# Who makes the sums of activation blocks for a Strassen-like down projection: VectorE or GpSimd

## Chip, cores and metric

The kernel runs on one core of a Trainium2 chip. The metric is the device time of one execution in microseconds (us). TensorE is called PE in the profile (its weight loads PEld), VectorE is DVE, ScalarE is ACT, GpSimd is POOL, SyncE is SP.

## What is computed

One decoder layer in float32, sequence 512, width 1024. Only its last part matters here, the feed-forward half:

```
h = rmsnorm(x);  u = causal depthwise conv3(h @ W_up)
a, b = split(u);  f = gelu(a) * b          # (512, 2816)
x = x + rmsnorm_post(f @ W_down)           # (2816 -> 1024)
```

## The kernel before, in words

**Products.** Every float32 operand of a matmul is split into a high half (rounded by ScalarE into a float32r tile) and a low half (operand minus high half, made by VectorE), and each product is three matmuls (L690 to L694). Both large feed-forward products are cut into 2 x 2 blocks and done with seven block products instead of eight, in a form in which sums and differences of blocks are built one after another. For the down projection the products are numbered 1 to 7. A unit is `(p, g)`: product `p` for the couple of feature tiles `g`, with g from 0 to 5. A couple has two pairs of tiles, the last couple (g = 5) one, so its units are half as long. There are 42 units in the hand-written order `DOWN_UNITS` (L82). The first four of them (`EARLY_DOWN`) stand among the last units of the up projection (`_tail`, L67).

**Weights.** A unit's weights go through one of six raw buffers. SyncE loads block 1 of a chain of sums by a plain transfer (L550, L556). The later members of a chain are made by transfers that add in flight onto what the buffer holds; these are issued from GpSimd's queue (L669 for the up projection, L677 for the down projection), each after VectorE has made the low half of the buffer's contents before (semaphore `w_lo`). ScalarE copies the raw buffer to one of four slots of `ws` (L1367, L1443, semaphore `w_hi`), VectorE subtracts (L1825 up, L1948 down, `w_lo`), TensorE multiplies and frees the slot (`unit_done`). The copies run four units ahead of TensorE.

**Activations.** `fT`, in the tile `work`, holds f in 22 tiles. A share is the operand of one unit, 128x512 (128x256 for g = 5): ScalarE writes its high half (L1434, `f_hi`), VectorE its low half (`f_share_lo`, L1921, `f_lo`). Before each unit TensorE waits for `w_lo` and `f_lo` (L1047, L1048). The operand of products 5, 6, 3 and 7 is not f itself but a sum or difference of blocks of f, built in place in `fT`. Four families of `tensor_tensor` on VectorE, six instructions each, make them:

- `f_difference(g)`, L1943, signals `f_diff`: before product 5;
- `f_sum_of` for p = 5, L1930, `f_sum2`: before product 6, and needed by the next two;
- `f_sum_of` for p = 6, L1934, `f_sum4`: before product 3;
- `f_sum_of` for p = 4, L1938, `f_sum3`: before product 7.

A sum of the last three families may overwrite a block only when the low half of the share before it has been made, so it waits for `f_lo`. `F_EARLY` and `F_DIFF` (L98, L101) say behind which unit of the up projection the first ones stand; `shares_at(n)` (L105) says which shares are split at step n of the down projection. VectorE's step n is: low half of weights n (`down_lo`), then the low halves and the sums of `shares_at(n)`.

**Orders.** Each engine runs its own list in order. GpSimd's list before: first all adding transfers of the up projection, then all of the down projection in the order of `DOWN_UNITS`, then four small row statistics at the end. All semaphores are waits on constants.

Of the kernel before, what the change touches and what calls it, by code (L numbers as in the profile page):

```python
# [32 lines left out]
ALU = mybir.AluOpType  # L33
# [10 lines left out]
FT = DFF // P  # L44
# [9 lines left out]
UP0 = OUT0 + 2 * KT  # L54
# [14 lines left out]
UP_UNITS = [("plain", 0, j) for j in range(4)] + [u for _, u in sorted(_steady, key=lambda e: e[0]) if u not in _tail] + _tail  # L69
UP_AT = {u: n for n, u in enumerate(UP_UNITS)}  # L70
EARLY_DOWN = 4
# [3 lines left out]
UP_ADDS = {7: (1, 0), 6: (1, 1), 3: (0, 1), 5: (1, 0)}  # L75
UP_NEXT = {1: 7, 7: 6, 6: 3, 4: 5}
DOWN0 = UP0 + len(UP_UNITS) - EARLY_DOWN
# [3 lines left out]
COUPLES = 6  # L81
DOWN_UNITS = [(1, 0), (1, 1), (1, 2), (5, 0), (1, 3), (5, 1), (6, 0), (1, 4), (5, 2), (1, 5), (5, 3),  # L82
# [10 lines left out]
STAGE = {p: (c, k) for c, stages in CHAINS.items() for k, (p, _) in enumerate(stages)}  # L93
# [7 lines left out]
F_DIFF = {(2, 4): 0, (2, 6): 1, (5, 7): 2, (5, 8): 3}  # L101
# [3 lines left out]
def shares_at(n):  # L105


    def upto(k):
        return min(9 if k < 9 else max(k, 10) + min(max(k - 11, 0) // 3, 6), len(DOWN_UNITS))

    return range(upto(n - 1), upto(n))
# [9 lines left out]
def raw_of(n):  # L121

    p, g = DOWN_UNITS[n]
    return (4, 5, 3, 0, 2, 1)[CHAIN_ORDER.index((STAGE[p][0], g)) % RAWS]
# [9 lines left out]
def down_n(k):  # L134

    return UP0 + UP_AT["down", k] if k < EARLY_DOWN else DOWN0 + k
# [10 lines left out]
def raw_slot_of(n):  # L147

    kind, i = unit_of(n)[:2]
    if kind == "in":  # L150
        return slot_of(n)
    if kind == "down":
        return raw_of(i)
    if kind == "plain":
        return unit_of(n)[2]
    if kind == 2:
        return 5
    return (2, 3)[i % 2] if kind in (4, 5) else (4, 0, 1)[(i - PLAIN) % 3]
# [13 lines left out]
def loads_of_slot(n):  # L172

    return sum(raw_slot_of(m) == raw_slot_of(n) and is_loaded(m) for m in range(n + 1))
# [7 lines left out]
def before_in_slot(n):  # L182

    return max((m for m in range(n) if raw_slot_of(m) == raw_slot_of(n)), default=None)
# [10 lines left out]
def lo_count(n):  # L195

    if n < POOL_TO:
        return n + 1
    return n + 1 - POOL_TO
# [15 lines left out]
def build(nc, x, norm_mix_pre, w_in, rel_bias, w_out, norm_mix_post, norm_ffn_pre, w_up,  # L215
          conv_w, conv_b, w_down, norm_ffn_post, rotary, decay, onehot, out):
    ctx = ExitStack()
    with ctx:
# [99 lines left out]
        def raw_unit(n):  # L318

            c = raw_of(n)  # L320
            return (late[:, c - 4, :] if c >= 4 else raw[:, c, :])[:, 0:512 * pairs_of(DOWN_UNITS[n][1])]
# [23 lines left out]
        def f_block(g, odd, half):  # L345

            t, w = 4 * g + odd, slice(half * 256, half * 256 + 256)
            return fT[:, t:t + 2 * pairs_of(g) - 1:2, w]
# [39 lines left out]
        raw_loaded = [sem(f"raw_loaded{s}") for s in range(RAWS)]  # L388
# [63 lines left out]
        def up_block(block, i):  # L452

            value, half = block
            return w_up_v[:, 4 * half:4 * half + 4, value * DFF + i * (2 * P):value * DFF + (i + 1) * (2 * P)]

        def up_raw(n):

            c = raw_slot_of(n)
            return late[:, c - 4, :] if c >= 4 else raw[:, c, :]  # L460

        def w_block(p, g):

            odd, right = BLOCK[p]
            t = 4 * g + odd
            return w_down_v[:, t:t + 2 * pairs_of(g) - 1:2, right * 512:right * 512 + 512]
# [101 lines left out]
        def _(pool):  # L568
# [87 lines left out]
            for pair in ((0, 1), (2, 3)):  # L656
                for s in pair:
                    out_rstd(s)
                for s in pair:
                    pool.wait_ge(sq_done, ST + s + 1)  # L660
                    row_rstd(ST + s, sumsq[:, ST + s:ST + s + 1])
            for n, unit in enumerate(UP_UNITS):
                if unit[0] not in UP_NEXT:
                    continue
                p, i = UP_NEXT[unit[0]], unit[1]
                m = UP0 + UP_AT[p, i]
                pool.wait_ge(raw_loaded[raw_slot_of(m)], 16 * loads_of_slot(m))
                pool.wait_ge(w_lo, lo_count(UP0 + n))
                pool.dma_start(up_raw(m).rearrange("p (k n) -> p k n", k=4), up_block(UP_ADDS[p], i),  # L669
                               accum_op=ALU.add).then_inc(raw_added[raw_slot_of(m)], 16)  # L670

            for n, (p, g) in enumerate(DOWN_UNITS):
                if not STAGE[p][1]:
                    continue
                c = raw_of(n)
                pool.wait_ge(w_lo, lo_count(before_in_slot(down_n(n))))
                pool.dma_start(raw_unit(n), w_block(p, g), accum_op=ALU.add).then_inc(raw_added[c], 16)  # L677

            for k, s in enumerate((2, 3, 0, 1)):
                pool.wait_ge(block_sq, (4, 6, 7, 8)[k])  # L680
# [841 lines left out]
        def _(dve):  # L1522
# [389 lines left out]
                nc.vector.tensor_tensor(t_block(p, 1), tF[m], f32(t_block(p, 0)), ALU.subtract).then_inc(t_lo, 1)  # L1912

            def f_lo_of(n):
                f_share_lo(n)
                f_sum_of(n)

            def f_share_lo(n):
                g = DOWN_UNITS[n][1]
                dve.wait_ge(f_hi, n + 1)  # L1920
                nc.vector.tensor_tensor(two(f_unit(n, 1), g), f_operand(n), f32(two(f_unit(n, 0), g)),  # L1921
                                        ALU.subtract).then_inc(f_lo, 1)

            def f_sum_of(n):
                p, g = DOWN_UNITS[n]
                a11, a12, a21, a22 = f_block(g, 0, 0), f_block(g, 1, 0), f_block(g, 0, 1), f_block(g, 1, 1)
                if p == 5:

                    dve.wait_ge(f_lo, n + 1)
                    nc.vector.tensor_tensor(a11, a21, a11, ALU.add).then_inc(f_sum2, 1)  # L1930
                if p == 6:

                    dve.wait_ge(f_lo, n + 1)
                    nc.vector.tensor_tensor(a21, a11, a12, ALU.subtract).then_inc(f_sum4, 1)  # L1934
                if p == 4:

                    dve.wait_ge(f_lo, n + 1)
                    nc.vector.tensor_tensor(a22, a11, a22, ALU.subtract).then_inc(f_sum3, 1)  # L1938

            def f_difference(g):  # L1940

                dve.wait_ge(f_ready, min(4 * g + 4, FT))
                nc.vector.tensor_tensor(f_block(g, 0, 1), f_block(g, 1, 1), f_block(g, 0, 1), ALU.subtract).then_inc(f_diff, 1)  # L1943

            def down_lo(n):
                c, w = slot_of(down_n(n)), 512 * pairs_of(DOWN_UNITS[n][1])
# [56 lines left out]
            for n in range(len(UP_UNITS)):  # L2003
                up_sum(n)
                if unit_of(UP0 + n + AHEAD)[0] == "down":
                    down_lo(unit_of(UP0 + n + AHEAD)[1])
                else:
                    up_split_lo(n + AHEAD)
                up_post(n)
                if n < 4:  # L2010
                    blocks_lo(n)
                if UP_UNITS[n] in F_DIFF:
                    f_difference(F_DIFF[UP_UNITS[n]])
                for m in F_EARLY.get(UP_UNITS[n], ()):
                    if n + 1 < len(UP_UNITS):
                        f_lo_of(m)
# [1 line left out]
            late_share, = F_EARLY[UP_UNITS[-1]]  # L2018
            gate_row(SWEEP - 1, 0)
            gate_row(SWEEP - 1, 1)  # L2020
            f_share_lo(late_share)
            for n in range(AHEAD + EARLY_DOWN, len(DOWN_UNITS)):
                if n == last[6] + 4:
                    e_sums()
                    g_sums()
                if n == AHEAD + EARLY_DOWN + 1:
                    f_tiles(SWEEP - 1)
                down_lo(n)
                if n == AHEAD + EARLY_DOWN + 2:
                    f_sum_of(late_share)  # L2030
                    f_difference(COUPLES - 2)
                if n == AHEAD + EARLY_DOWN + 4:
                    f_difference(COUPLES - 1)
                for m in shares_at(n):
                    f_lo_of(m)
                if n == last[4] + 3:
                    e4_sums()
                    dve.wait_ge(gains3_loaded, 16)
                if n == last[3] + 4:
                    for r in range(2):  # L2040
                        dve.wait_ge(g_done, r + 1)
                        add_block(r, 1, 3, g_sum)
                if n == last[3] + 5:
                    gain(0, 1)
                    gain(1, 1)
                if n == last[7] + 3:
                    for r in range(2):
                        dve.wait_ge(e4_done, r + 1)
                        add_block(2 + r, 0, 7, e_sum)
                        add_block(2 + r, 1, 7, g_sum)  # L2050
                if n == last[7] + 4:
                    gain(2, 0)
                    gain(2, 1)
                if n == last[7] + 5:
                    gain(3, 0)
                    gain(3, 1)
# [60 lines left out]
```

## Time and profile before

| | |
|---|---|
| median of 3 runs | 619.94 us (619.67 to 621.11) |
| the profiled execution | 619.47 us |
| its span in the trace | 617.7 us |
| TensorE busy | 606.2 us, 98% |
| VectorE busy | 473.8 us, 77% |
| ScalarE busy | 364.9 us, 59% |
| GpSimd busy | 143.9 us, 23% |

The up projection's seven-product part runs from about 289 us to 515 us of the span, the down projection from there to 612 us (its first four units lie between 499 and 513 us). The last microseconds are the norm and the stores. A row of a timeline gives start and duration in us, engine, line of the kernel, operation, tiles and shapes; in brackets the idle time of that engine before it and what ended it. Instructions of one engine that follow without a gap overlap by some hundredths of a microsecond, so the distance between two starts is what an instruction takes of its engine's time.

### The profile page before, as it was taken

Reading aid. Unit: us, or ns where it says so; the run is one execution under the profiler, and the core shown is the slowest. Engines: PE = TensorE matmul, PEld = TensorE weight load, DVE = VectorE, ACT = ScalarE, POOL = GpSimd, SP = SyncE. Lnnn points to the kernel's source line nnn. Section 1 sums busy time; section 2 is a strip of 40 time slices with the busy share of each in tenths; the row PEclk is TensorE's granted clock in tenths of the full one; section 3 lists DMA queues with packets and bytes.
Section 4 is the critical chain, followed back from the end, with each engine's and each line's share of the span. In section 5 each row is a group of like instructions: output and inputs, shape, how many; then the busy total and the mean of one; then the engine's idle time right before and its main releaser. Section 6 shows DMA issues by size and latency. Waiting matters only on the chain.

```text
span 617.7 us, 9966 instructions
## 1 busy us (share of the span) xinstructions
PE 606.2 (98%) x3710; PEld 531.5 (86%) x3710; DVE 473.8 (77%) x678; ACT 364.9 (59%) x571; POOL 143.9 (23%) x145
## 2 busy tenths in 40 slices
PE   8999999999999999999999999999999999899996
PEld 8888778788787877889989999999999998688885
DVE  3657548656854985978974598889889899999886
ACT  5558337536743853773844566666666656667661
POOL 4313103111310302312012222222222322522213
PEclk9999999999999999999999999999999999999998
DMA  9834223322422255581467988998899879997933
GB/s 278 239 103 126 86 69 103 102 58 78 135 69 68 102 179 165 186 254 35 103 157 151 177 158 178 210 186 172 154 222 184 184 141 183 162 235 175 233 103 136
DMA packets 87785, 93.27 MB, mean 151 GB/s; under 512 B 3049, under 2 KB 72345, under 8 KB 87746
## 3 DMA queue, kind: packets, MB, share of 16 engines
q0 software_dynamic: 26352, 35.15, 33.6%
q1 hardware_dynamic: 61394, 57.59, 29.2%
q8 instruction: 25, 0.41, 0.3%
q14 instruction: 14, 0.11, 0.1%
HBM read 90.62 MB, written 2.12 MB: 150 GB/s over the span
## 4 chain that ended last, share of the span: by engine, by line
PE 84%; DVE 8%; POOL 2%; issue 2%; ACT 2%; DMA 1%; DVEq 0%; SPq 0%; POOLq 0%; ACTq 0%
PE bank L694 75%; DVE ws L1948 2%; PE bank L774 1%; PE bank L836 1%; PE bank L705 1%; POOL grstd L622 1%; DMA gains<-in_norm_mix_pre_dram 1%; PE bank L825 1%; DVE xs L1649 1%; PE bank L765 1%; PE bank L764 1%; POOL work L626 1%; PE bank L815 1%; DVE work L1819 1%; PE bank L814 1%
## 5 line engine op out<-in xcount | busy, mean ns | idle before, releaser
L694 PE MATMUL bank<-hT,ws 128*128 128x256 f32 (+1 forms) x1656 | 295.3, 332 | 0.7 <-DVE work L1627 0.6
L694 PEld LDWEIGHTS bank<-hT,ws 128*128 128x128 f32 x1656 | 245.7, 190 | 28.2 <-issue 2.5
L694 PE MATMUL bank<-yT,ws 128*128 128x256 f32 x864 | 106.8, 283 | 0.0
L694 PEld LDWEIGHTS bank<-yT,ws 128*128 128x128 f32 x864 | 105.2, 192 | 0.2
L694 PE MATMUL bank<-ws,yT 128*128 128x512 f32 x366 | 86.6, 392 | 2.1 <-DVE yT L1921 2.1
L694 PEld LDWEIGHTS bank<-ws,yT 128*128 128x128 f32 x366 | 67.8, 188 | 16.6 <-DVE ws L1948 2.5
L1367 ACT ACTIVATE ws<-raw 128x1024 fp32r<-128x1024 f32 x46 | 48.7, 1059 | 46.1 <-PE bank L694 46.1
L1825 DVE TENSOR_TENSOR ws<-raw,ws 128x1024 fp32r<-128x1024 f32 x46 | 56.1, 1221 | 15.2 <-ACT ws L1367 15.2
L1529 DVE TENSOR_TENSOR ws<-raw,ws 128x1024 fp32r<-128x1024 f32 x47 | 57.6, 1226 | 5.8 <-ACT ws L1105 5.4
L669 POOL DMA_DIRECT2D raw<-in_w_up_dram x27 | 34.7, 1284 | 108.1 <-DVE ws L1825 103.6
L1105 ACT ACTIVATE ws<-raw 128x1024 fp32r<-128x1024 f32 x48 | 50.7, 1058 | 14.9 <-PE bank L694 10.8
L694 PE MATMUL bank<-ws,hT 128*128 128x512 f32 x240 | 55.6, 389 | 0.0
L694 PEld LDWEIGHTS bank<-ws,hT 128*128 128x128 f32 x240 | 44.9, 188 | 9.2
L1825 DVE TENSOR_TENSOR ws<-late,ws 128x1024 fp32r<-128x1024 f32 x21 | 25.7, 1222 | 16.0 <-ACT ws L1367 16.0
L1443 ACT ACTIVATE ws<-raw 128x1024 fp32r<-128x1024 f32 (+1 forms) x28 | 26.6, 950 | 15.6 <-PE bank L694 14.8
L1367 ACT ACTIVATE ws<-late 128x1024 fp32r<-128x1024 f32 x21 | 22.3, 1060 | 21.9 <-PE bank L694 21.4
L1649 DVE CUSTOM_DVE_ANT_0 xs<-bank,work 128x128 f32<-128x128 f32 (+3 forms) x32 | 14.7, 489 | 25.6 <-PE bank L815 25.4
L1948 DVE TENSOR_TENSOR ws<-raw,ws 128x1024 fp32r<-128x1024 f32 (+1 forms) x28 | 30.4, 1084 | 3.8 <-ACT ws L1443 3.8
L1597 DVE TENSOR_TENSOR work<-bank,work 128x512 f32<-128x512 f32 (+3 forms) x32 | 15.5, 489 | 19.9 <-PE bank L765 19.9
L677 POOL DMA_DIRECT2D raw<-in_w_down_dram x16 | 18.5, 1176 | 33.2 <-DVE ws L1948 33.2
L669 POOL DMA_DIRECT2D late<-in_w_up_dram x9 | 11.7, 1297 | 52.8 <-DVE ws L1825 52.8
L1175 ACT ACTIVATE work<-bank 32x512 f32<-32x512 f32 x32 | 18.9, 591 | 8.5 <-PE bank L694 8.1
(174 smaller groups left out, 794.5 us busy)
## 6 DMA issues: line engine op xcount, KB each, us to landing
raw<-in_w_in_dram SPq DMA_DIRECT2D x28, 512.0 KB, 4.0
raw<-in_w_up_dram POOLq DMA_DIRECT2D x27, 512.0 KB, 6.4
raw<-in_w_up_dram SPq DMA_DIRECT2D x23, 512.0 KB, 5.9
raw<-in_w_out_dram SPq DMA_DIRECT2D x16, 512.0 KB, 3.4
late<-in_w_up_dram SPq DMA_DIRECT2D x12, 512.0 KB, 5.9
raw<-in_w_down_dram POOLq DMA_DIRECT2D x12, 512.0 KB, 7.6
late<-in_w_up_dram POOLq DMA_DIRECT2D x9, 512.0 KB, 6.0
raw<-in_w_down_dram SPq DMA_DIRECT2D x9, 512.0 KB, 4.4
```

The costliest lines, as they stand in the source:

```text
L669: pool.dma_start(up_raw(m).rearrange("p (k n) -> p k n", k=4), up_block(UP_ADDS[p], i), accum_op=ALU.add).then_inc(raw_added[raw_slot_of(m ...
L677: pool.dma_start(raw_unit(n), w_block(p, g), accum_op=ALU.add).then_inc(raw_added[c], 16)
L694: return nc.tensor.matmul(dst, st, mv, start=start, stop=stop, skip_group_check=onto)
L1105: nc.scalar.activation(ws[:, c, 0, :], raw[:, c, :], ACT.Copy).then_inc(w_hi, 1)
L1175: ins = nc.scalar.activation(rots[32 * b:32 * b + 32, :], bank[UNIT_BANK[j]][src:src + 32, :], ACT.Copy)
L1367: nc.scalar.activation(ws[:, c, 0, :], up_raw(UP0 + n), ACT.Copy).then_inc(w_hi, 1)
L1443: nc.scalar.activation(ws[:, c, 0, 0:w], raw_unit(n), ACT.Copy).then_inc(w_hi, 1)
L1529: nc.vector.tensor_tensor(ws[:, c, 1, :], raw[:, c, :], f32(ws[:, c, 0, :]), ALU.subtract).then_inc(w_lo, 1)
L1597: nc.vector.tensor_tensor(retp[:, h, packed(mt):packed(mt) + width(mt)], bank[S_BANK[u % 2]][:, 0:width(mt)], dtab[:, h, 0:width(mt)], ALU ...
L1649: nc.vector.tensor_tensor_reduce(out=probs[:, u % 4, 0:w], in0=bank[S_BANK[u % 2]][:, 0:w], in1=btab[:, h, 0:w], scale=-0.125, scalar=3.0e ...
L1825: nc.vector.tensor_tensor(ws[:, c, 1, :], up_raw(UP0 + n), f32(ws[:, c, 0, :]), ALU.subtract).then_inc(w_lo, 1)
L1948: nc.vector.tensor_tensor(ws[:, c, 1, 0:w], raw_unit(n), f32(ws[:, c, 0, 0:w]), ALU.subtract).then_inc(w_lo, 1)
```

## The change

The four families of sums leave VectorE's list and stand in GpSimd's. `AHEAD` is 4. GpSimd's list becomes one loop over units in VectorE's order: at each step the adding transfers that wait for that step's low half of weights, and then the sums of that step. So an adding transfer of the down projection is now issued in the order of the low half that frees its buffer, not in the order of `DOWN_UNITS`. VectorE keeps the low halves of the shares. The waits of consumers (ScalarE's L1427 to L1433) stay as they are.

```
 GpSimd:
-            for n, unit in enumerate(UP_UNITS): ... (L662 to L670: adding transfers, up)
-            for n, (p, g) in enumerate(DOWN_UNITS): ... (L672 to L677: adding transfers, down)
+            def add_after(n):
+                if n < UP0 + len(UP_UNITS) and UP_UNITS[n - UP0][0] in UP_NEXT:
+                    p, i = UP_NEXT[UP_UNITS[n - UP0][0]], UP_UNITS[n - UP0][1]
+                    m = UP0 + UP_AT[p, i]
+                    pool.wait_ge(raw_loaded[raw_slot_of(m)], 16 * loads_of_slot(m))
+                    pool.wait_ge(w_lo, lo_count(n))
+                    pool.dma_start(up_raw(m)..., up_block(UP_ADDS[p], i), accum_op=ALU.add)...
+                for m, (p, g) in enumerate(DOWN_UNITS):
+                    if STAGE[p][1] and before_in_slot(down_n(m)) == n:
+                        pool.wait_ge(w_lo, lo_count(n))
+                        pool.dma_start(raw_unit(m), w_block(p, g), accum_op=ALU.add)...
+            def f_difference(g):
+                pool.wait_ge(f_ready, min(4 * g + 4, FT))
+                nc.gpsimd.tensor_tensor(f_block(g, 0, 1), f_block(g, 1, 1), f_block(g, 0, 1), ALU.subtract).then_inc(f_diff, 1)
+            def f_sum_of(n):
+                p, g = DOWN_UNITS[n]
+                a11, a12, a21, a22 = f_block(g, 0, 0), f_block(g, 1, 0), f_block(g, 0, 1), f_block(g, 1, 1)
+                if p == 5:
+                    pool.wait_ge(f_lo, n + 1)
+                    pool.wait_ge(f_diff, g + 1)
+                    nc.gpsimd.tensor_tensor(a11, a21, a11, ALU.add).then_inc(f_sum2, 1)
+                if p == 6:
+                    pool.wait_ge(f_lo, n + 1)
+                    pool.wait_ge(f_sum2, g + 1)
+                    nc.gpsimd.tensor_tensor(a21, a11, a12, ALU.subtract).then_inc(f_sum4, 1)
+                if p == 4:
+                    pool.wait_ge(f_lo, n + 1)
+                    pool.wait_ge(f_sum2, g + 1)
+                    nc.gpsimd.tensor_tensor(a22, a11, a22, ALU.subtract).then_inc(f_sum3, 1)
+            AHEAD = 4
+            for n in range(AHEAD):
+                add_after(UP0 + n)
+            for n in range(len(UP_UNITS)):
+                add_after(UP0 + n + AHEAD)
+                if UP_UNITS[n] in F_DIFF:
+                    f_difference(F_DIFF[UP_UNITS[n]])
+                for m in F_EARLY.get(UP_UNITS[n], ()):
+                    f_sum_of(m)
+            for n in range(AHEAD + EARLY_DOWN, len(DOWN_UNITS)):
+                add_after(DOWN0 + n)
+                if n == AHEAD + EARLY_DOWN + 2:
+                    f_difference(COUPLES - 2)
+                if n == AHEAD + EARLY_DOWN + 4:
+                    f_difference(COUPLES - 1)
+                for m in shares_at(n):
+                    f_sum_of(m)
 VectorE:
             def f_lo_of(n):
-                f_share_lo(n)
-                f_sum_of(n)
                 (the body of f_share_lo; f_sum_of and f_difference go)
...
-                if UP_UNITS[n] in F_DIFF:
-                    f_difference(F_DIFF[UP_UNITS[n]])
...
-            f_share_lo(late_share)
+            f_lo_of(late_share)
...
-                if n == AHEAD + EARLY_DOWN + 2:
-                    f_sum_of(late_share)
-                    f_difference(COUPLES - 2)
-                if n == AHEAD + EARLY_DOWN + 4:
-                    f_difference(COUPLES - 1)
```

## Rows read from the trace of the kernel before

**Rows 1.** The page's first part: span, and busy time of each engine.

```profile
span 617.7 us, 9966 instructions
PE 606.2 (98%) x3710; PEld 531.5 (86%) x3710; DVE 473.8 (77%) x678; ACT 364.9 (59%) x571; POOL 143.9 (23%) x145
```

**Rows 2.** Windows: stretch, its length, then busy us of PE, PEld, DVE, ACT, POOL.

```profile
528.00:565.00 37.00, 34.86 (x154) 28.43 (x153) 36.06 (x51) 25.77 (x39) 12.21 (x11) 1.00 0.99 201
532.70:611.80 79.10, 79.03 (x348) 65.16 (x348) 73.08 (x101) 48.12 (x77) 20.57 (x19) 1.00 0.77 177
```

**Rows 3.** Waits of TensorE from 350 us on: us in total, times, longest.

```profile
PE bank L694 <- DVE yT L1921: 2.1, 1, 2.1
```

**Rows 4.** The chain that ended last: start, us, what.

```profile
494.48 0.69 DVE work L1930
...
506.91 0.61 DVE hT L1921
...
529.68 0.60 DVE work L1930
530.28 0.60 DVE work L1943
...
532.02 0.61 DVE yT L1921
532.76 79.24 PE bank L694 x348
```

**Rows 5.** Timeline of VectorE in the down projection.

```profile
524.01 0.68 DVE L1921 TENSOR_TENSOR yT<-work,yT 128x512 fp32r<-128x512 f32 x1
524.61 1.22 DVE L1948 TENSOR_TENSOR ws<-raw,ws 128x1024 fp32r<-128x1024 f32 x1
...
539.13 0.68 DVE L1921 TENSOR_TENSOR yT<-work,yT 128x512 fp32r<-128x512 f32 x1
539.84 0.69 DVE L1934 TENSOR_TENSOR work<-work 128x512 f32<-128x512 f32 x1
540.45 0.42 DVE L1921 TENSOR_TENSOR yT<-work,yT 128x256 fp32r<-128x256 f32 x1
540.91 0.42 DVE L1930 TENSOR_TENSOR work<-work 128x256 f32<-128x256 f32 x1
541.25 1.22 DVE L1948 TENSOR_TENSOR ws<-raw,ws 128x1024 fp32r<-128x1024 f32 x1
...
563.68 1.22 DVE L1948 TENSOR_TENSOR ws<-raw,ws 128x1024 fp32r<-128x1024 f32 x1
```

**Rows 6.** Groups of VectorE, 289 to 565 us: the four families of sums.

```profile
L1934 DVE TENSOR_TENSOR work<-work 128x512 f32<-128x512 f32 (+1 forms) x6 | 3.9, 648 | 0.2
L1938 DVE TENSOR_TENSOR work<-work 128x512 f32<-128x512 f32 (+1 forms) x6 | 3.9, 648 | 0.2
L1930 DVE TENSOR_TENSOR work<-work 128x512 f32<-128x512 f32 (+1 forms) x6 | 3.9, 646 | 0.2
L1943 DVE TENSOR_TENSOR work<-work 128x512 f32<-128x512 f32 (+1 forms) x6 | 3.8, 639 | 0.0
```

**Rows 7.** Timeline in the mixer: GpSimd's additions L626 and VectorE beside them.

```profile
101.77 1.29 POOL L626 TENSOR_TENSOR work<-work 128x512 f32<-128x512 f32 x1
101.82 1.79 DVE L1622 TENSOR_TENSOR work<-work,grstd 128x512 f32<-128x512 f32 x1
...
245.66 0.69 DVE L1622 TENSOR_TENSOR work<-work,grstd 128x512 f32<-128x512 f32 x1 [1.82 <-POOL grstd L622]
...
56.26 1.22 DVE L1529 TENSOR_TENSOR ws<-raw,ws 128x1024 fp32r<-128x1024 f32 x1
56.49 2.12 POOL L626 TENSOR_TENSOR work<-work 128x512 f32<-128x512 f32 x1 [3.87 <-DVE work L1668]
```

**Rows 8.** Timeline of TensorE: units 21 to 24 of the down projection.

```profile
560.15 9.68 PE L694 MATMUL bank<-ws,hT 128*128 128x512 f32 x42
```

**Rows 9.** DMA issues of the page: count, KB each, us from issue to landing.

```profile
raw<-in_w_down_dram POOLq DMA_DIRECT2D x12, 512.0 KB, 7.6
```

More of the change, by code:

```diff
@@ L661, in _ @@
                     row_rstd(ST + s, sumsq[:, ST + s:ST + s + 1])
[L662 to L677, printed above, removed]
+            def add_after(n):
[4 more added lines that the diff above has]
+                    pool.wait_ge(w_lo, lo_count(n))
+                    pool.dma_start(up_raw(m).rearrange("p (k n) -> p k n", k=4), up_block(UP_ADDS[p], i),
+                                   accum_op=ALU.add).then_inc(raw_added[raw_slot_of(m)], 16)
+                for m, (p, g) in enumerate(DOWN_UNITS):
+                    if STAGE[p][1] and before_in_slot(down_n(m)) == n:
+                        pool.wait_ge(w_lo, lo_count(n))
+                        pool.dma_start(raw_unit(m), w_block(p, g), accum_op=ALU.add).then_inc(raw_added[raw_of(m)], 16)
@@ L1914, in f_lo_of @@
             def f_lo_of(n):
-                f_share_lo(n)
-                f_sum_of(n)
-            def f_share_lo(n):
                 g = DOWN_UNITS[n][1]
@@ L1922, in f_share_lo @@
                                         ALU.subtract).then_inc(f_lo, 1)
[L1924 to L1943, printed above, removed]
             def down_lo(n):
```

## The prediction

> **What bounds the kernel now.** I read the busy times first: TensorE is busy 606.2 of 617.7 us [rows 1], so only time in which it stands still can be won. The view of waits shows how much of it there is where the change works: from 350 us on TensorE waits once, 2.1 us, for VectorE's low half of a share, L1921 [rows 3]. The chain that ended last says why: from about 490 us to 532 us it runs almost wholly through VectorE, and three of its links are instructions that the change takes away (L1930 at 494.48 and 529.68, L1943 at 530.28); a fourth, a sum of L1934, stands right behind the low half at 506.91. At 532.76 TensorE begins unit 10 and never stops again for 79 us [rows 4]: 79.03 of 79.10 us busy [rows 2]. So VectorE is late exactly once. But from 528 to 565 us VectorE itself is busy 36.06 of 37 us [rows 2]: it just keeps up. Its low half for unit 23 ends at 563.68 + 1.22 = 564.9 [rows 5]; TensorE's units 21 to 24 start at 560.15, at 9.68 / 42 = 0.23 us a matmul, so unit 23, behind 24 matmuls, starts at 565.7 [rows 8]. VectorE's lead there is 0.8 us. Two numbers bound the outcome: at most 2.1 us can be won, and 0.8 us of delay is free.
>
> **What the change removes.** Four families of six sums, 0.64 us each by mean [rows 6], 15.5 us of VectorE. Six in each family make 24: per family five of 128x512 and one of 128x256. Five come early (four differences and the sum of share 3, before 475 us), where VectorE waits for ScalarE each turn and TensorE never waits for it; I cost those at nothing, covered by that idle time. Two (behind shares 5 and 6) lie in the chain between 494 and 508 us. Seventeen lie between 528 and 561 us, 13 full and 4 half.
>
> In VectorE's time a sum is worth more than its own pitch. Share, sum, next share: 539.13, 539.84, 540.45, so 1.32 us; a share with no sum behind it: 524.01 to 524.61, 0.60 us [rows 5]. Removed: 0.72 us each, as the sum also waited for the share's own end. For a half one: 540.45 to 541.25 is 0.80 us, less 0.34 (540.91 to 541.25) for the half share alone: 0.46. The differences and the sum of share 8 didn't follow their share, and give 0.60 (a half one 0.34). In the stretch that is 11 x 0.72 + 2 x 0.60 + 3 x 0.46 + 0.34 = 10.8 us; with the two before, 1.4 us, it is 12.3 us in all.
>
> **What it adds.** The sums are 1.29 us each on GpSimd, by the addition L626, the same operation, shape and type [rows 7]. GpSimd has the room: 12.2 of 37 us busy [rows 2], plus 13 x 1.29 and 4 halves at about 0.7, is 32 us.
>
> The price lies on VectorE. At 101.77 GpSimd begins L626; at 101.82 VectorE begins L1622, two operands from SBUF, and takes 1.79 us. The same instruction takes 0.69 us where GpSimd does nothing (245.66) [rows 7]. It ends 0.55 us after GpSimd's end: it stood still while GpSimd worked. The other way round, L1529 holds from 56.26 to 57.48, and GpSimd's addition that began at 56.49 takes 2.12 us, ending 1.13 us after VectorE's end [rows 7]. So an addition of GpSimd and a VectorE instruction with two SBUF operands exclude each other, 1.10 us per full addition, whoever comes first. After the change VectorE's list in this stretch is almost nothing but such instructions: low halves of weights (raw and ws) and of shares (work and the high half). Only what reads a bank is exempt.
>
> I take 1.09 us of standstill per full sum. The bounds: above, the full 1.29 us (0.65 for a half one), 3.4 us more in the sum below; below, zero, for a sum that falls into a wait of VectorE. With VectorE busy 36 of 37 us the upper end is nearer. No row has a 128x256 addition on GpSimd; its bounds are zero and 1.09, and I take half, 0.55.
>
> The Trainium skill (SBUF — State Buffer, Who interferes with whom) has the shared pair of ports as an exclusive lock held for the whole instruction. The row shows 1.10 of 1.29 us. By the whole instruction the sum below would come out at its upper bound, near 628 us.
>
> **The sum.** Standstill: 15 full sums x 1.09 + 4 x 0.55 = 18.6 us. The last half sum, behind share 24, meets the two bank-reading subtractions of L1961 and costs nothing: 18.0. Less what VectorE no longer does, 12.3: VectorE reaches the low half of unit 23 by 5.7 us later. Less the lead of 0.8 us: TensorE's unit 23 starts 4.9 us later. Behind it no sum is left, and VectorE's list is shorter than TensorE's, so the 4.9 us stay as they are: TensorE's later work and the tail move whole. 619.47 + 4.9 = 624.4; the median lies 0.5 us above the profiled execution, so I say 624.5 us.
>
> Latencies elsewhere: GpSimd's sum waits for `f_lo`, and behind it on GpSimd stand the next adding transfers, for which ScalarE's copies of weights wait. They land 7.6 us after issue [rows 9]. A raw buffer comes round after five units, about 13.7 us; issue, 7.6 us, a high and a low half of about 1.2 us each make 10 to 11 us, so some 3 us are free, and one blocked sum ahead costs 2.1. I cost this at nothing; if the cover goes it is the second rival. The new order of the transfers lets some go earlier (that of unit 16 no longer waits for units 10 to 15), but nothing waits for them: nothing. ScalarE gets its sums one to four steps later than they are made, so 1.3 instead of 0.6 us is hidden too.
>
> **Rivals.**
> - *No standstill in this stretch* (the other side). If GpSimd's sums fall beside bank-reading instructions and VectorE's waits, VectorE is freed by 2.6 us up to unit 10 (1.4 and the 1.2 us at 529.68), more than the 2.1 us of TensorE's wait: it closes, and 617.3 us result. It decides at the wait before unit 10. For it: GpSimd's idle time. Against it: rows 7, and that each sum is released by the end of a share's low half, when VectorE mostly has its next two-operand low half ready. Break-even is at a standstill of (12.3 + 0.8) / 16.5 = 0.79 us per full sum, the full gain at about 0.66. Chance 0.11.
> - *Partly hidden*, standstill 0.7 to 0.95 us: 618 to 621.8 us. Chance 0.14.
> - *Transfers late besides.* GpSimd has 32 of 37 us of work and waits for `w_lo`, `f_lo` and VectorE's end in between. If a transfer stands behind two blocked sums (4.2 us), more than the 3 us that are free, each round of the raw buffers gains about 1.2 us, and with the upper bound of the standstill (3.4 us) the end is at 628 to 634 us. Chance 0.15.
>
> **How the numbers follow.** The forecast case (standstill about 1 to 1.3 us, 621.8 to 628) gets 0.60. A measurement of this kernel can tell 0.3%, 1.9 us, from no change. Slower by more: 0.60 + 0.15 = 0.75; same 0.14; faster 0.11. The range takes the forecast case, most of the partly hidden one and the lower half of the late transfers: 619.5 to 631.
>
> **What would show it.** After: the waits of TensorE between 515 and 570 us sum to about 7 us (2.1 now) in many small pieces for L1921 and L1948's successors. VectorE's low halves of 1.22 and 0.68 us show in part as 2.3 and 1.8 us while their distance to GpSimd's sums is nil. GpSimd's sums show 1.3 us alone and up to 2.4 us when second. Wrong if VectorE's low halves keep 1.22 and 0.68 us; if TensorE's one wait closes; or if ScalarE's copies of weights begin to wait for transfers (then the late transfers). A time under 618 refutes the standstill as a cost.

## The result and the profile after

The changed kernel takes 630.65 us (median of 6 runs, 629.83 to 631.24); the kernel before took 619.96 us in the same job (6 runs, 619.4 to 621.11). The ratio is 1.0168, with a 95% interval of 1.0155 to 1.0181: slower by 10.7 us. The forecast was 624.5 us, 4.5 us slower, within 619.5 to 631. The direction came out as forecast and the time lies at the top end of the range; the delay is more than twice the 4.5 us that were forecast. The profiled execution took 629.83 us.

The page after, its first part and the issue row of the adding transfers:

```profile
span 628.0 us, 9984 instructions
PE 609.4 (97%) x3710; PEld 531.3 (85%) x3710; DVE 486.8 (78%) x654; ACT 363.8 (58%) x571; POOL 178.4 (28%) x169
...
raw<-in_w_down_dram POOLq DMA_DIRECT2D x12, 512.0 KB, 6.0
```

VectorE has 24 instructions fewer than in [rows 1] and is busy 13.0 us longer: the removed work came back as longer instructions. GpSimd is busy 34.5 us longer. TensorE did the same 3710 matmuls and waits more. The transfers land in 6.0 us, not later than in [rows 9]. The view of waits, TensorE from 300 us to the end (total, times, longest):

```profile
PE bank L733 <- DVE ws L1962: 3.8, 4, 1.4
PE bank L733 <- DVE yT L1956: 3.7, 2, 3.5
PE bank L733 <- ACT late L1426: 1.0, 1, 1.0
PE bank L733 <- DVE gains L1888: 0.7, 2, 0.4
```

Instead of the one wait of 2.1 us in [rows 3] there is one of 3.5 us before unit 10, five smaller ones for VectorE's low halves around it (two before, three behind), two of 0.3 to 0.4 us for `gains` at 472.59 and 514.08, and one of 1.0 us for ScalarE at 491.08. The forecast had none of the last three. The timeline of VectorE after (L1956 is the low half of a share, L1962 and L1864 that of weights):

```profile
490.48 1.23 DVE L1864 TENSOR_TENSOR ws<-raw,ws 128x1024 fp32r<-128x1024 f32 x1 [0.25 <-ACT ws L1406]
...
534.64 2.30 DVE L1956 TENSOR_TENSOR yT<-work,yT 128x512 fp32r<-128x512 f32 x1
...
538.00 1.76 DVE L1956 TENSOR_TENSOR yT<-work,yT 128x512 fp32r<-128x512 f32 x1
539.68 3.77 DVE L1962 TENSOR_TENSOR ws<-raw,ws 128x1024 fp32r<-128x1024 f32 x1
...
574.48 1.21 DVE L1962 TENSOR_TENSOR ws<-raw,ws 128x1024 fp32r<-128x1024 f32 x1
```

and of GpSimd after, beside it:

```profile
533.88 1.20 POOL L674 DMA_DIRECT2D raw<-in_w_down_dram  x1 [1.21 <-DVE ws L1962]
534.62 1.77 POOL L679 TENSOR_TENSOR work<-work 128x512 f32<-128x512 f32 x1
...
537.03 2.18 POOL L688 TENSOR_TENSOR work<-work 128x512 f32<-128x512 f32 x1
539.16 1.19 POOL L674 DMA_DIRECT2D raw<-in_w_down_dram  x1
539.94 1.18 POOL L679 TENSOR_TENSOR work<-work 128x256 f32<-128x256 f32 x1
540.63 1.74 POOL L693 TENSOR_TENSOR work<-work 128x512 f32<-128x512 f32 x1
```

A share's low half is 0.68 us and that of weights 1.22 us where nothing disturbs them [rows 5]. At 538.00 the low half takes 1.76 us, 1.08 more, beside one sum. At 539.68 it takes 3.77 us, 2.55 more, and ends at 543.45, 1.08 us after the second of two sums of GpSimd that follow each other has ended at 542.37: VectorE stood still for both, the half one and the full one behind it. At 534.64 it takes 1.62 us more beside a single full sum; why that is more than 1.09 us is a question of its own below. I call such an excess a stop. The stops between 490 and 576 us sum to 20.9 us, between 289 and 490 us to 7.3 us, 28.2 us together (the expectations below, which count them a little shorter, have 27.9). Before the change no instruction of VectorE between 289 and 576 us was lengthened.

### The profile page after: what moved, and what is told of

It is laid out like the page before. It is cut to its first block, busy times and chain, and to the rows that moved or that the text cites. A ratio compares the mean times of both kernels' runs of the same rounds, so it can differ in the third digit from the quotient of the medians.

```text
span 628.0 us, 9984 instructions
## 1 busy us (share of the span) xinstructions
PE 609.4 (97%) x3710; PEld 531.3 (85%) x3710; DVE 486.8 (78%) x654; ACT 363.8 (58%) x571; POOL 178.4 (28%) x169
## 4 chain that ended last, share of the span: by engine, by line
PE 72%; DVE 18%; issue 3%; ACT 3%; POOL 2%; DMA 1%; DVEq 0%; SPq 0%; POOLq 0%; ACTq 0%
PE bank L733 63%; DVE ws L1962 5%; DVE ws L1864 2%; PE bank L875 1%; PE bank L813 1%; DVE hT L1956 1%; DVE yT L1956 1%; PE bank L744 1%; POOL grstd L622 1%; DMA gains<-in_norm_mix_pre_dram 1%; DVE work L1858 1%; PE bank L864 1%; DVE gains L1842 1%; DVE rot L1832 1%; DVE xs L1688 1%
## 5 line engine op out<-in xcount | busy, mean ns | idle before, releaser
L733 PE MATMUL bank<-ws,yT 128*128 128x512 f32 x366 | 88.8, 398 | 4.3 <-DVE yT L1956 3.7
L1864 DVE TENSOR_TENSOR ws<-raw,ws 128x1024 fp32r<-128x1024 f32 x46 | 58.8, 1279 | 12.8 <-ACT ws L1406 12.8
L1568 DVE TENSOR_TENSOR ws<-raw,ws 128x1024 fp32r<-128x1024 f32 x47 | 57.2, 1220 | 5.8 <-ACT ws L1144 5.3
L1144 ACT ACTIVATE ws<-raw 128x1024 fp32r<-128x1024 f32 x48 | 50.7, 1058 | 13.8 <-PE bank L733 10.8
L1864 DVE TENSOR_TENSOR ws<-late,ws 128x1024 fp32r<-128x1024 f32 x21 | 30.3, 1441 | 17.0 <-ACT ws L1406 17.0
L1962 DVE TENSOR_TENSOR ws<-raw,ws 128x1024 fp32r<-128x1024 f32 (+1 forms) x28 | 35.9, 1283 | 3.5 <-ACT ws L1482 3.5
L1482 ACT ACTIVATE ws<-raw 128x1024 fp32r<-128x1024 f32 (+1 forms) x28 | 26.5, 948 | 18.7 <-PE bank L733 18.6
L674 POOL DMA_DIRECT2D raw<-in_w_down_dram x16 | 18.5, 1157 | 20.9 <-DVE ws L1962 20.9
L1377 ACT ACTIVATE rot<-bank,conv 128x512 f32<-128x512 f32 x22 | 16.1, 772 | 14.4 <-DVE bank L1870 10.4
```

What stands on the lines that cost most here:

```text
L674: pool.dma_start(raw_unit(m), w_block(p, g), accum_op=ALU.add).then_inc(raw_added[raw_of(m)], 16)
L733: return nc.tensor.matmul(dst, st, mv, start=start, stop=stop, skip_group_check=onto)
L1144: nc.scalar.activation(ws[:, c, 0, :], raw[:, c, :], ACT.Copy).then_inc(w_hi, 1)
L1377: nc.scalar.activation(ca[:, r, :], src, ACT.Identity, scale=tap(2 * i + r, 2), bias=tap(2 * i + r, 3)).then_inc(gtap2, 1)
L1482: nc.scalar.activation(ws[:, c, 0, 0:w], raw_unit(n), ACT.Copy).then_inc(w_hi, 1)
L1568: nc.vector.tensor_tensor(ws[:, c, 1, :], raw[:, c, :], f32(ws[:, c, 0, :]), ALU.subtract).then_inc(w_lo, 1)
```

## The experiments

All the kernels below come from the changed one. In them each of the 24 sums can stand in either engine's list: `ON_POOL` names those that GpSimd makes, as `("f", g)` for the difference of couple g and `("s", n)` for the sum behind share n. A sum waits for the same events as in the two kernels, and in addition for the one before it of its family where that one is made on the other engine. All have the new order of the adding transfers. `PLACED` holds a sum back until the low half of weights of a given step is done, and puts it before that step's transfers. In these kernels a share's low half is L1983, weights' low halves are L1889 (up) and L1991 (down), a sum is L455, an adding transfer of the down projection L714, a matmul L758. The 95% interval of a ratio stands in brackets.

**First set: which part costs?** The order of transfers alone:

```
+ON_POOL = []
```

> Only the new order of GpSimd's adding transfers; all 24 sums are back on VectorE. Theory A (an addition on GpSimd and a two-operand VectorE instruction exclude each other) and theory B (the sums come late because GpSimd's list is long): both 620.0 us, within 0.6. Theory C (the new order of the transfers costs the time): 625 or more, with ScalarE waiting for transfers.

Measured: 619.87 us against 619.89, ratio 1.0002 [0.9987, 1.0017]. The new order of the transfers costs and brings nothing. The whole change is the sums.

The five early sums alone, and the 19 later ones alone:

```
+ON_POOL = [("f", 0), ("f", 1), ("f", 2), ("f", 3), ("s", 3)]     # early
+ON_POOL = [("f", 4), ("f", 5)] + [the 17 sums behind share 3]    # late
```

> New order, and only the five early sums (four differences, the sum of share 3) on GpSimd. As recorded before (covered by VectorE's idle time, costs nothing): 620.0 us. Theory A as the changed kernel's trace reads: VectorE is stopped five times by 1.0 to 1.7 us, arrives 1.9 us late at 490 us, and since it is the chain from there on TensorE's wait before unit 10 grows by as much: 621.5 to 622.5 us. B: 620.0, as those sums have no consumer waiting.

> New order, the 19 late sums on GpSimd, the five early ones on VectorE. A: the changed kernel's 630.7 less the 1.9 us that VectorE arrives late at 490 us: 628 to 629.5 us; VectorE's instructions from 490 to 576 us together stretched by 20 us. B: no change against the changed kernel, 630.7.

Measured: early 623.11 us, 1.0055 [1.0033, 1.0077]; late 627.41 us, 1.0127 [1.0104, 1.0151]. 3.2 and 7.5 us are together 10.7 us, the whole change. The five that I had costed at nothing cost 3.2. The late ones alone have stops of 20.9 us, as many as in the change. Each time lies 0.6 us outside its expectation, the early one above and the late one below: the lateness at 490 us had been taken as 1.9 us and is larger (third set).

**Is it the reading?** The same list with each sum replaced by two writes of zeros to the same block, together 1.06 us against the 1.29 us of a full sum (this kernel leaves out the sums; the later products are computed from zeros):

```
-engine.tensor_tensor(out, a, b, op).then_inc(signal, 1)
+engine.memset(out, 0.0).then_inc(again, 1)
+q.wait_ge(again, times[0])
+engine.memset(out, 0.0).then_inc(signal, 1)
```

> The changed kernel with every sum on GpSimd replaced by two memsets of the same block, one after the other (it leaves out the sums: the operands of products 5, 6, 3 and 7 are zeros): same waits, same place in the list, about 1.1 us each on GpSimd, but nothing read from SBUF. A with an exclusion of reads: VectorE's low halves keep 1.22 and 0.68 us, TensorE's wait before unit 10 closes, 617.5 to 618.5 us. If writes exclude too: near 628. B: near 628 to 630, as GpSimd's list is as long as before.

Measured: 616.65 us, 0.9949 [0.9931, 0.9967], 0.9 us below the expectation. Its timeline, GpSimd and then VectorE (L1990 a share's low half, L1998 that of weights):

```profile
528.52 1.03 POOL L460 MEMSET work<- 128x512 f32 x1
529.61 0.53 POOL L462 MEMSET work<- 128x512 f32 x1
```

```profile
528.56 0.69 DVE L1990 TENSOR_TENSOR yT<-work,yT 128x512 fp32r<-128x512 f32 x1
529.39 1.23 DVE L1998 TENSOR_TENSOR ws<-raw,ws 128x1024 fp32r<-128x1024 f32 x1
530.53 0.68 DVE L1990 TENSOR_TENSOR yT<-work,yT 128x512 fp32r<-128x512 f32 x1
```

GpSimd works at the same places, and every low half of VectorE keeps its 0.68 and 1.22 us. From 300 us on TensorE does not wait at all. So it is not GpSimd's waits, nor its queue, nor the order of its work: it is GpSimd's reading of SBUF while VectorE wants two operands from it. About 3.2 us is also what the move would have brought had there been no exclusion; this is an estimate, as the writes are shorter than the sums and the later products work on zeros. The Trainium skill (SBUF — State Buffer, Who interferes with whom) says that a VectorE instruction with two SBUF inputs contends with a GpSimd instruction that reads SBUF and not with one that only writes it. The stops of the changed kernel agree with the first half, this trace with the second.

**Second set: placing.** The sums before the transfers of each step, instead of behind them, to see whether the larger stops come from a sum right behind a transfer's issue:

```
 for n in range(AHEAD + EARLY_DOWN, len(DOWN_UNITS)):
-    add_after(DOWN0 + n)
     ... the differences and sums of step n ...
+    add_after(DOWN0 + n)
```

The same exchange is made in the loop over the units of the up projection.

> The changed kernel with the two parts of each of GpSimd's steps exchanged: first the sums of the step, then its adding transfers. Theory A1 (a sum that is dispatched while GpSimd still issues the transfer before it stops VectorE for that issue's rest too, which is why some stops lasted 1.3 to 1.7 us instead of 1.09): no stop above 1.15 us per full sum, all stops from 289 to 576 us together 22 to 24 us instead of 27.9, and 626 to 628.5 us. Rival A2 (the long stops come from the place of the sum in VectorE's list, or from two sums in a row): stops as long as before, 630.7 or more. Rival D (transfers have little time to spare): ScalarE waits for transfers, 631 or more.

Measured: 628.13 us, 1.0121 [1.0105, 1.0137]. The stops did not shrink as expected (27.7 us against 28.2 over the whole); a difference still fell behind the transfer of the step before it, and its low half of weights took 3.12 us. Where a single full sum stood behind a share the stop was about 1.1 us. Against the kernel before of its own job it is 7.2 us slower, where the change is 10.7. 1.7 us of that gain are TensorE's waits for ScalarE and for `gains`, 1.0 of them at 491 us, which are gone; the rest has no cause shown. For the question asked this run decides nothing.

Then only the three sums that lie in the chain before unit 10 [rows 4], each held until VectorE is at rows of the causal convolution, which read a bank and one operand from SBUF:

```
+ON_POOL = [("s", 5), ("s", 6), ("f", 4)]
+PLACED = {down_n(2): [("s", 5)], down_n(7): [("s", 6), ("f", 4)]}
```

> Only three sums on GpSimd (behind shares 5 and 6, and the difference of couple 4), each held back until VectorE has finished the low half of weights (unit 2; unit 7) behind which it works on the gate rows, whose instructions read a bank and one SBUF operand; the other 21 on VectorE. Theory A: no stop on VectorE above 0.2 us, VectorE 2.0 us earlier before unit 10, TensorE's wait there shrinks from 2.1 to 0.1 to 0.4 us, and the time is 618.0 us (617.6 to 618.6). If every addition of GpSimd stops every VectorE instruction with an SBUF operand: stops of about 1.1 us, 621 to 622. If the wait before unit 10 has another cause: 619.9.

and the same three without being held:

```
+ON_POOL = [("s", 5), ("s", 6), ("f", 4)]
+PLACED = {}
```

> The same three sums on GpSimd, but in the places of the changed kernel, right behind what releases them. Theory A: stops of 1.0, 1.1 and 1.1 to 1.6 us, less the 2.0 us that VectorE is freed of: the wait before unit 10 grows by 1 to 2 us, 621.0 to 622.0. If the place doesn't matter: the same as with the three held back.

Measured: held 617.50 us, 0.9947 [0.9934, 0.9960], 3.5 us less than before and the fastest kernel of this study that makes the sums. Not held: 623.56 us, 1.0042 [1.0031, 1.0054], 1.6 us above its expectation. The same three instructions on the same engine differ by 6.1 us by where they stand. GpSimd in the held kernel:

```profile
502.92 1.29 POOL L455 TENSOR_TENSOR work<-work 128x512 f32<-128x512 f32 x1 [5.18 <-DVE ws L1991]
...
520.51 2.55 POOL L455 TENSOR_TENSOR work<-work 128x512 f32<-128x512 f32 x2 [1.77 <-DVE ws L1991]
```

VectorE beside the first of them, and TensorE at unit 10, of the same kernel:

```profile
502.74 0.74 DVE L1857 SCALAR_TENSOR_TENSOR rot<-bank,conv,rot 128x511 f32<-128x511 f32 x1
503.52 0.75 DVE L1860 SCALAR_TENSOR_TENSOR rot<-bank,conv,rot 128x510 f32<-128x510 f32 x1
504.19 1.22 DVE L1991 TENSOR_TENSOR ws<-late,ws 128x1024 fp32r<-128x1024 f32 x1
```

```profile
531.38 15.32 PE L758 MATMUL bank<-ws,yT 128*128 128x512 f32 x66 [0.44 <-DVE yT L1983]
```

Both engines run at full speed side by side: sums of 1.29 us, nothing on VectorE stretched. TensorE's wait is 0.44 us where it was 2.1 [rows 3]. VectorE's instructions beside the other two sums (520.34 to 523.3 us) keep their 0.74 and 0.75 us as well. In the kernel that does not hold them, GpSimd and VectorE:

```profile
530.91 1.20 POOL L714 DMA_DIRECT2D raw<-in_w_down_dram  x1 [1.22 <-DVE ws L1991]
531.65 1.76 POOL L455 TENSOR_TENSOR work<-work 128x512 f32<-128x512 f32 x1
```

```profile
531.14 3.37 DVE L1991 TENSOR_TENSOR ws<-late,ws 128x1024 fp32r<-128x1024 f32 x1
```

The low half of 1.22 us takes 3.37, a stop of 2.15 us for one sum. The sum has nothing to wait for (its inputs were long there) and stands right behind a transfer's issue that is still running until 532.11; the trace has the sum from 531.65 on, 1.76 us long. The three stops are 0.98, 1.09 and 2.15 us, 4.2 in all, more than the 2.0 us of VectorE's work that went, and TensorE's wait grew from 2.1 to 4.0 us. The kind of instruction that is met does not explain the 2.15 us: in the changed kernel a low half of weights at 566.26, beside a sum with no issue ahead of it, is stopped for 1.09 us.

**Third set: the early five, and the stop of 2.15 us.** Two of the five, then the other three:

```
+ON_POOL = [("f", 0), ("f", 1)]
+ON_POOL = [("f", 2), ("f", 3), ("s", 3)]
```

> Only the differences of couples 0 and 1 on GpSimd (at 364 and 404 us of the trace), in the changed kernel's places. Theory E1 (an early stop is free when VectorE's idle time until its next critical stretch makes up for it): two stops of 1.7 us, VectorE on time at 490 us, 620.3 us as without them. Theory E2 (each early stop costs its full excess over the 0.6 us that is saved): 622.5 us.

> Only the differences of couples 2 and 3 and the sum of share 3 on GpSimd (453 to 475 us). E1: they lie within 40 us of the stretch in which VectorE is the chain, with too little idle time between: VectorE 1.9 us late at 490, TensorE waits there too, and all of the cost of the five shows: 623.0 to 623.8 us. E2: 622.0 us (three fifths of 3.2 on 620.3).

Measured: 619.79 us, 0.9992 [0.9979, 1.0004], and 623.71 us, 1.0044 [1.0027, 1.0061]. The first two, at 364 and 404 us, have stops of 1.7 us each and cost nothing: the idle time that I had named covers them. The three between 453 and 475 us carry the whole price. There VectorE works toward the end of the up projection. Its low half of weights at the end of it, in the two kernels:

```profile
487.88 1.23 DVE L1889 TENSOR_TENSOR ws<-raw,ws 128x1024 fp32r<-128x1024 f32 x1 [0.78 <-ACT ws L1431]
```

```profile
491.28 1.23 DVE L1889 TENSOR_TENSOR ws<-raw,ws 128x1024 fp32r<-128x1024 f32 x1 [0.25 <-ACT ws L1431]
```

Before the change this instruction stood at 488.63, after it at 490.48, with only 0.25 us of idle time ahead of it. Executions differ in where their up projection begins (TensorE's first matmul of the part from 289 us on is at 289.56 before, 288.74 after, 288.80 with the first two, 289.56 with the other three); counted from there VectorE is late by 2.67 us in the change, by 2.65 with the three, and by nothing with the two. So the lateness of three sums is carried over the border of the two projections.

Why the idle time is no cover there can be read at the third sum. ScalarE and VectorE in the kernel with the three:

```profile
473.33 1.52 ACT L1409 ACTIVATE gains<-gains,conv 128x512 f32<-128x512 f32 x2 [2.00 <-DVE gains L1913]
475.83 2.81 DVE L1889 TENSOR_TENSOR ws<-late,ws 128x1024 fp32r<-128x1024 f32 x1 [1.46 <-ACT ws L1431]
```

and the same two instructions before the change:

```profile
471.52 1.52 ACT L1345 ACTIVATE gains<-gains,conv 128x512 f32<-128x512 f32 x2 [0.20 <-DVE gains L1849]
474.23 1.23 DVE L1825 TENSOR_TENSOR ws<-late,ws 128x1024 fp32r<-128x1024 f32 x1 [1.05 <-ACT ws L1367]
```

VectorE begins its low half 1.60 us late and still has waited 1.46 us for ScalarE's copy, more than the 1.05 us of before: ScalarE had first waited 2.00 us for VectorE, and the copy stands behind that in its list. Over 440 to 492 us ScalarE's waits for VectorE grow from 2.4 to 13.4 us. The idle time moved with the delay instead of taking it up.

TensorE's waits from 300 us on are 4.0 us in both kernels that have the three (2.1 before), so they are 1.9 of the 3.2 and 3.3 us. In the traced executions of both its clock also fell behind the wait before unit 10, and in that of before it did not (last section); that price isn't measured apart here.

The kernel with three sums again, with the last of them held until the next step's low half, so that it does not stand behind a running issue:

```
 ON_POOL = [("s", 5), ("s", 6), ("f", 4)]
-PLACED = {}
+PLACED = {down_n(11): [("f", 4)]}
```

> The run with the three sums in the changed kernel's places, but the difference of couple 4 is held back until VectorE has finished the low half of weights of unit 11, long after GpSimd's transfer issue before it has ended. Theory A1 (a sum that has nothing to wait for takes the exclusion while the transfer issue before it still runs): its stop on VectorE falls from 2.15 to 1.1 us, the first wait of TensorE from 4.0 to about 2.5 us as the stop now falls behind share 10's turn, and the time to 622 to 622.8 us. A2 (the length of the stop comes from the instruction of VectorE that it meets): 2.1 us again, no change of the time.

Measured: 621.16 us, 1.0013 [1.0003, 1.0023], 0.8 us below the expectation. That is 2.4 us less than without holding by the two medians, and 1.9 us less (0.7 against 2.6) if each is counted from the kernel before of its own job. GpSimd and VectorE at that sum:

```profile
531.37 1.20 POOL L714 DMA_DIRECT2D raw<-in_w_down_dram  x1 [1.21 <-DVE ws L1991]
532.91 1.65 POOL L455 TENSOR_TENSOR work<-work 128x512 f32<-128x512 f32 x1 [0.33 <-DVE ws L1991]
```

```profile
533.45 1.66 DVE L455 TENSOR_TENSOR work<-work 128x512 f32<-128x512 f32 x1
```

Now the sum waits for VectorE, begins 0.34 us after the issue has ended (531.37 + 1.20 = 532.57), and VectorE's stop is 0.98 us. TensorE's wait went from 4.0 to 1.9 us. So a stop has two parts: about 1.1 us for the sum itself, and up to 1.2 us more (2.15 - 0.98) if the sum is handed over while the transfer before it is still being issued. The second part is what is left of the issue when VectorE begins its instruction. Nine such stops by a single full sum follow one line. With 0.17 us of the issue left the stop is 1.36 us (453.27 of the changed kernel), with 0.39 to 0.48 left it is 1.59 to 1.66 (364.02, 404.34, 475.03, 534.64 and 544.58), with 0.67 and 0.68 left 1.88 (471.29 in the kernel with the sums first, 542.96 in the last one below), with 0.97 left 2.15. Each is 1.18 to 1.21 us more than that rest. Where VectorE's next instruction begins only after the issue's end, the stop is 1.10 us (551.93 and 563.95 of the changed kernel, sums recorded from 551.35 and 562.98 on). So VectorE stands still for the rest of the issue and then for the sum.

At last all 24 sums, with each of the six differences (the ones that have nothing to wait for) held in this way:

```
 ON_POOL = EARLY_SUMS + LATE_SUMS
+PLACED = {UP0 + 26: [("f", 0)], UP0 + 40: [("f", 1)], UP0 + 56: [("f", 2)], UP0 + 63: [("f", 3)],
+          down_n(11): [("f", 4)], down_n(13): [("f", 5)]}
```

> All 24 sums on GpSimd as in the changed kernel, but each of the six differences is held back until a later low half of weights, so that none is dispatched behind a running transfer issue. A1: the six stops fall to about 1.1 us (0.55 for the half one), all stops from 289 to 576 us together from 27.9 to 24.5 to 25.5 us, and 628 to 629.7 us. A2: 27.9 us of stops and 630.7 us.

Measured: 628.23 us, 1.0117 [1.0100, 1.0134]. The stops fell from 28.2 to 23.9 us, those of the four early differences from 1.4 to 1.7 us each to 0.5 to 0.9. Holding wins 2.9 us of the 10.7, each counted from the kernel before of its own job (2.4 by the two medians). Of the stops that are left about 1.5 us still come from sums behind a share that follow an issue (at 542.96 one of 1.88 us); the rest is about 1.09 us per full sum and stays, because GpSimd makes the sums where VectorE's list has only instructions with two operands from SBUF.

## Why the prediction was right or wrong

**Right: the bound and the mechanism.** VectorE's low halves do set TensorE's start at unit 10 and at unit 23, and moving the sums cost more than it freed through the exclusion of [rows 7]. The kernel with writes alone shows it: same places, no stops, 3.2 us faster than before.

**Right: the size of one stop.** 1.09 us for a full sum was taken; a full sum released by a share shows 1.08, and a half one 0.54 us (at 561.67 a share's low half takes 1.22 instead of 0.68 us) where 0.55 was taken as the middle of its bounds. "Up to 2.4 us" for a sum that comes second: 2.18 at 537.03. The Trainium skill (SBUF — State Buffer, Who interferes with whom) has the lock held for the whole instruction, which would be 1.29 us; the stops are 1.08, as the rows said. For how long the ports themselves are held the durations do not tell.

**Right: the order and the latency of the transfers cost nothing.** The kernel with the new order alone is at 1.0002, and in the changed kernel ScalarE never waits for a transfer. That the range holds the time is luck: its upper end was put at 631 for the late transfers, which did not come. The rival "transfers late besides" would have given the right number (628 to 634 us) by the wrong way.

**Wrong, the first term: the early sums "costed at nothing".** The step read that VectorE waits for ScalarE each turn up to 475 us and took that idle time for cover. It is cover at 364 and 404 us. At 453 to 475 us it no longer is: ScalarE, for which VectorE waits, itself waits for VectorE there and comes late with it (1.46 us of idle time at 475.83 with VectorE 1.60 us late). The chain through VectorE begins at about 490 us [rows 4], and of the idle time before its low half there, 0.79 us before the change, 0.25 us is left after it. Three sums cost 1.59 + 0.99 + 1.36 = 3.9 us of stops and left VectorE 2.67 us late at 490 us. The text had named no end of that cover, and gave the term no upper bound.

**Wrong, the second term: the standstill in the stretch, 18.0 us.** It measured 20.9 us. Of the 2.9 us more, 2.5 are the stops of 1.62 us and the like that the transfers' issues lengthen. 0.4 is the last half sum, at 572.18, which was put at nothing: it meets L1982, which has two operands from SBUF, and not only the bank-reading pair ahead of it, and lengthens it from 0.68 to 1.10 us. [rows 7] has additions without an issue ahead of them, so no row of before showed this; the bound of 1.29 us per sum contained it (21.4 us for the stretch), but for another reason.

**The sum, remade.** Late at 490 us 2.67, stops 20.9, saved 12.3 (as forecast), a wait for ScalarE of about 0.3 us that was not there before (at 496.56): VectorE reaches unit 23's low half 11.6 us late by this account. The trace has 574.48 instead of 563.68, 10.8 us, and 11.6 counted from the start of the up projection's part. Less the lead of about 0.7 us, TensorE's unit 23 is 10.9 us late (start 575.75 less 565.67, and the 0.8 us by which the two executions differ at 289 us), and the median is 10.7 us late. Forecast for that place: 4.9. Of the 6.0 us in between, 2.7 are the early sums, 2.5 the lengthened stops, 0.4 the last half sum, and 0.4 the smaller terms. The forecast's last line also lost 0.3 us: the median before and the 4.9 us make 624.8, not 624.5.

**Forecast of the waits.** TensorE's waits between 515 and 570 us were to sum to about 7 us in many small pieces. They are 6.2 us there (3.7 for shares, 2.4 for weights) and 1.4 at 575.75, in six pieces, the longest 3.5 us. TensorE also waited 1.7 us before 515 us (1.0 of it at 491.08). All its idle time grew by 7.1 us (18.6 against 11.5 by the two pages). Its busy time grew by 3.2 us: the clock fell (below), and what lengthened it beyond that is not shown.

**The rivals.** "No standstill in this stretch" needed sums beside instructions that read a bank. That is not how the change places them, but it can be had: with three sums placed there the time is 3.5 us below that of before, where the rival's working gave 2.1 (the wait). The rest fits the clock (last section), which is not shown apart.

## What to carry to other kernels

Before a two-operand SBUF instruction is moved from VectorE to GpSimd, list what VectorE does at the moment in which it will run there: beside instructions that read a bank it is free; beside instructions with two SBUF operands it costs VectorE 1.09 us for a 1.29 us sum, more than the 0.60 to 0.72 us that it frees. Move only the few that lie on the chain, hold them with a wait until VectorE's harmless stretch, and do not let one stand directly behind a transfer's issue. And if idle time is named as cover, look up where it ends, what hangs on the engine right behind that point, and whether the engine that ends the idle time itself waits for the one that is to be delayed.

## What was unexpected in the hardware

**A stop that begins in a transfer's issue.** Up to 2.15 us of standstill on VectorE for one 1.29 us sum. That the place behind the issue matters is shown by the held kernel, 2.15 to 0.98 us. What in the issue holds VectorE is open: the issue alone, with no sum behind it, never lengthened an instruction of VectorE between 289 and 576 us in the kernel before, nor did an issue with writes behind it.

**TensorE's clock after a short wait.** The windows of two kernels with practically the same program, the kernel before and the one with the new order of transfers alone, from unit 10 on (busy us of PE, PEld, DVE, ACT, POOL, then the granted clock, DMA share, GB/s). Before:

```profile
532.76:536.50 3.74, 3.73 (x16) 2.98 (x17) 3.71 (x6) 2.55 (x6) 1.72 (x2) 1.00 1.07 158
```

New order alone:

```profile
533.10:536.80 3.70, 3.70 (x9) 2.93 (x10) 3.67 (x6) 1.72 (x4) 1.93 (x2) 0.54 0.96 170
```

And TensorE's rows that begin there, before and new order alone:

```profile
532.76 15.30 PE L694 MATMUL bank<-ws,yT 128*128 128x512 f32 x66 [2.14 <-DVE yT L1921]
```

```profile
533.09 16.86 PE L758 MATMUL bank<-ws,yT 128*128 128x512 f32 x66 [2.15 <-DVE yT L1983]
```

The engine stood still for 2.14 and 2.15 us before. In the first execution it goes on at 2.4 GHz; in the second the mean granted clock of 3.7 us is 0.54, so it is at the lower level of 1.2 GHz for nearly all of them, only 9 matmuls fit instead of 16, and the 66 take 1.56 us longer. That fits the spread of the kernel before: of its 19 runs in the last set 9 lie between 618.7 and 620.0 us and 10 between 620.4 and 621.4. The runs have no trace each, so this is a reading and not shown; the three traced executions with such a wait and no other change of time agree with it (no fall: 619.47 us, before; fall: 621.74 us, new order alone, and 620.54 us, two early sums). In the kernels whose wait there is 0.4 us (three sums held) or none (writes alone) the clock stays at 1.00, and they gain more (3.5 and 3.2 us) than the 2.1 us of the wait that they close. The Trainium skill (TensorE: Matmul & The Clock Gate, Why this matters for your kernels) names idle gaps between bursts as what drops the clock; here a fall follows a gap of 2.15 us in one execution and no fall one of 2.14 us in another. Over all traces of this case the clock falls after waits of 1.89 us (three sums, one held), 2.15 (twice), 2.49, 2.52 and 3.48 to 4.04 us, and stays after 0.44, 1.88 (all sums, differences held) and 2.14 us. Why the one and not the other stays open. In the changed kernel the clock falls too (0.79 in 536 to 544 us), but VectorE is the later one there, so I put no separate price on it.
